# A seventh buffer for expert weights, and another order of layer 0's expert blocks

## What is computed

```python
gi = argmax(softmax(h @ wg + bg)); le = logits of the 8 experts of group gi
tw, ti = top_k(softmax(le), 2); weight = max(pg) * tw / sum(tw); expert = gi * 8 + ti
# for each expert e, over the tokens that chose it, in blocks of 128 rows:
gate, up = split(h[idx] @ w_gu[e], 2)        # 1024 -> 512 + 512
y = (silu(gate) * up) @ w_down[e]            # 512 -> 1024
x = x + g2 * sum over the token's two experts of weight * y
```

## Time and profile before

| | us |
|---|---|
| median of three runs | 2635.58 |
| profiled execution | 2634.51 |
| its span | 2632.6 |
| TensorE matmul busy | 2505.9 (95%) |
| VectorE busy | 1501.1 (57%) |
| POOL busy | 457.7 (17%) |
| matmuls of line 2734: busy, idle before them | 1020.6, 55.4 |
| queue q1, share of 16 engines' span | 51.7% |
| queue q0 | 4.3% |

### The profile page before, as it was taken

The page is one execution under the profiler, slowest core; times in us unless marked ns, Lnnn a source line. Parts: engine busy times, 40 slices in busy tenths (PEclk is TensorE's granted clock), DMA queues, the critical chain, the costliest instruction groups (busy, mean ns, idle before and its releaser), DMA issues.

```text
span 2632.6 us, 33966 instructions
## 1 busy us (share of the span) xinstructions
PE 2505.9 (95%) x12794; PEld 1241.2 (47%) x12794; DVE 1501.1 (57%) x3270; ACT 562.4 (21%) x1181; POOL 457.7 (17%) x527
## 2 busy tenths in 40 slices
PE   6999999999999998999999899999999999999888
PEld 3444456647755533333333344577745433333333
DVE  3264347228778765555555566677787754354435
ACT  3211111118722100000000231488821000000002
POOL 0043200203011132222220012000011122222202
PEclk9999999999999999999999999899999999999999
DMA  9710111114032799999999810300024799999997
GB/s 379 306 26 0 68 49 39 58 22 104 14 142 82 293 392 423 423 382 404 421 408 382 329 49 1 72 2 1 2 75 160 282 402 421 420 413 421 419 406 282
DMA packets 101998, 590.73 MB, mean 224 GB/s; under 512 B 23742, under 2 KB 27078, under 8 KB 76872
## 3 DMA queue, kind: packets, MB, share of 16 engines
q1 hardware_dynamic: 81832, 535.74, 51.7%
q0 software_dynamic: 17408, 43.34, 4.3%
q10 hardware_dynamic: 2592, 9.44, 0.9%
HBM read 555.00 MB, written 45.99 MB: 228 GB/s over the span
## 4 chain that ended last, share of the span: by engine, by line
PE 77%; DMA 14%; DVE 5%; issue 2%; SPq 1%; POOL 0%; ACT 0%; POOLq 0%; DVEq 0%; ACTq 0%
PE PS L2734 28%; PE PS L1072 11%; DMA ar<-in_expert_w_gu_dram 9%; PE PS L1924 5%; PE PS L1268 5%; PE PS L1936 4%; PE PS L1947 4%; PE PS L2157 4%; PE PS L1458 4%; PE PS L1741 4%; DMA ar<-yd 1%; DMA h2d<-ar 1%; PE PS L2150 1%; PE PS L651 1%; DMA ar<-in_ada_w_dram 1%
## 5 line engine op out<-in xcount | busy, mean ns | idle before, releaser
L2734 PE MATMUL PS<-ar 128*32 128x512 f32 (+2 forms) x4608 | 1020.6, 602 | 55.4 <-DMA ar<-in_expert_w_gu_dram 41.9
L2734 PEld LDWEIGHTS PS<-ar 128*32 128x32 f32 (+2 forms) x4608 | 386.3, 138 | 685.5 <-issue 672.2
L1072 PE MATMUL PS<-ar 128*128 128x512 f32 (+1 forms) x768 | 313.9, 565 | 4.2 <-DMA ar<-in_swa_w_in_dram 2.5
L2949 DVE TENSOR_TENSOR ar<-PS,ar 128x512 f32<-128x512 f32 x48 | 33.1, 690 | 485.6 <-ACT ar L2875 485.6
L2963 DVE STREAM_TRANSPOSE ar<-ar 32x128 f32<-32x128 f32 x736 | 296.1, 402 | 10.9
L2875 ACT ACTIVATE ar<-PS 128x512 f32<-128x512 f32 x48 | 28.7, 597 | 1049.8 <-PE PS L2734 1049.8
L1072 PEld LDWEIGHTS PS<-ar 128*128 128x128 f32 x768 | 144.2, 192 | 150.2 <-issue 141.2
L3050 POOL DMA_INDIRECT ar<-h2d,ar x176 | 177.4, 1008 | 140.4 <-DVE ar L2652 57.4
L1980 DVE CUSTOM_DVE_ANT_0 ar<-PS,ar 128x640 f32<-128x640 f32 (+2 forms) x208 | 158.1, 797 | 71.8 <-PE PS L1924 71.7
L2157 PE MATMUL PS<-ar 128*128 128x512 f32 x392 | 175.2, 597 | 1.5 <-ACT ar L2288 0.9
L3058 POOL DMA_INDIRECT yd<-ar x47 | 48.7, 1035 | 711.9 <-DVE ar L2981 699.9
(11 more groups left out here) (349 smaller groups left out, 2452.5 us busy)
## 6 DMA issues: line engine op xcount, KB each, us to landing
ar<-in_expert_w_gu_dram SPq DMA_DIRECT2D x128, 2048.0 KB, 18.2
ar<-in_expert_w_down_dram SPq DMA_DIRECT2D x64, 2048.0 KB, 17.3
ar<-in_ada_w_dram SPq DMA_DIRECT2D x24, 2048.0 KB, 14.7
ar<-yd SPq DMA_DIRECT2D x36, 512.0 KB, 5.6
ar<-in_ab_w_in_dram SPq DMA_DIRECT2D x6, 2048.0 KB, 9.2
h2d<-ar ACTq DMA_DIRECT2D x18, 512.0 KB, 2.8
ar<-in_x_dram SPq DMA_DIRECT2D x8, 512.0 KB, 13.2
ar<-in_ab_w_out_dram SPq DMA_DIRECT2D x1, 4096.0 KB, 30.6
```

What stands on the lines that cost most here:

```text
L1072: mm = nc.tensor.matmul(out_, lhs, rhs, start=(k == 0), stop=(k == KC - 1))
L2734: mm = nc.tensor.matmul(out[at:to], lhsT[:, at:to], w[:, k, cols], start=start, stop=stop)
```

## The change

- `piece_at` gets a seventh buffer at `WR`, where `hb`, `hbT` and a part of `sg` lay. `hb` and `yb` are left with one buffer each, `gub` is dropped and its product is written over `sg`; `yb` lies at `TR`.
- So `gather_quarters(b)` waits for the transpose of b-1 instead of b-2, and `result(b)` for the scatter of b-1 instead of b-2. The gather of block 1 waits until block 0's rows are turned on TensorE. silu waits for the transposes out of `sg` (`guT`) instead of the product (`mul`).
- Layer 0's order becomes WWpqqqWqqqWqqqWpWWWqqqWpW. Layer 1's is unchanged.
- Block 1's down piece is fetched before block 2's gate piece, so seven pieces can be placed by hand (`FIRST`) before the planner takes over; SyncE loads pieces 2 to 5 of layer 0 (1 to 4 before) ahead of the ranks, and 3 to 5 of layer 1 (3 and 4 before).
- The four halves of modulation weights at layer 0's end go into other buffers and wait for other products, in the queue's order: the first one product earlier than before, the second and third one later, the fourth as before. `fix_rows` also waits for the last transpose out of `hb`.

The core of the diff:

```diff
@@ -89,6 +89,10 @@
     rest = [whole(r, 2 + pairs + shared * mains + r - c) for r in range(c, EXP)]
+    if l == 0:
+        take = dict(pair=iter(groups[:pairs]), four=iter(groups[pairs:]), one=iter([[r] for r in rest]))
+        order = ["pair", "four", "one", "four", "one", "four", "one", "pair", "one", "one", "one", "four", "one", "pair", "one"]
+        return first + [x for kind in order for x in next(take[kind])]
     seq = first + groups[0]
@@ -281,16 +285,17 @@
 
-        piece_at = [SLOT1, SLOT1 + 4096, SLOT1 + 8192, SLOT0, SLOT0 + 4096, SLOT0 + 8192]
-        hb = [R(WR + 1024 * i, D) for i in range(2)]
+        piece_at = [SLOT1, SLOT1 + 4096, SLOT1 + 8192, SLOT0, SLOT0 + 4096, SLOT0 + 8192, WR]
+        RING = len(piece_at)
+        FIRST = ((2, 6, 0, 1, 5, 3, 4), (0, 1, 2, 3, 4, 6, 5))
+        hb = R(WR + 4096, D)
         srcq = R(51456, 4 * EXP)
...
         h2q = h2d.rearrange("t (a n) -> (t a) n", a=4)
-        hbT = [R(WR + 2048 + 1024 * i, D).rearrange("p (k n) -> p k n", k=KC) for i in range(2)]
-        sg = [R(WR + 4096 + 512 * i, 512) for i in range(2)]
-        gub = [R(WR + 5120 + 512 * i, 512) for i in range(2)]
+        hbT = [R(WR + 5120 + 1024 * i, D).rearrange("p (k n) -> p k n", k=KC) for i in range(2)]
+        sg = [R(WR + 7168 + 512 * i, 512) for i in range(2)]
         guT = [R(TR + 3072 + 512 * i, 512).rearrange("p (k n) -> p k n", k=4) for i in range(2)]
-        yb = [R(WR + 6144 + 1024 * i, D) for i in range(2)]
+        yb = R(TR, D)
 
...
@@ -348,10 +353,11 @@
                 self.l, self.n = l, f"m{l}"
-                self.blocks, self.pieces, self.at, self.fills = moe_blocks(l), [], {}, [0] * 6
+                self.blocks, self.pieces, self.at, self.fills = moe_blocks(l), [], {}, [0] * RING
                 nb, known = len(self.blocks), {}
                 for b in range(nb + 1):
-                    for part, k in (("g", b), ("d", b - 1), ("u", b)) if l == 1 and b == nb - 1 else (("g", b), ("u", b), ("d", b - 1)):
+                    for part, k in (("g", b), ("d", b - 1), ("u", b)) if l == 1 and b == nb - 1 else (("g", b), ("u", b), ("d", b - 1)) if b != 2 else \
+                            (("d", b - 1), ("g", b), ("u", b)):
                         if not 0 <= k < nb:
@@ -361,7 +367,7 @@
                             self.at.setdefault((part, k), []).append((i, lo, hi))
-                held = [None] * 6
+                held = [None] * RING
 
@@ -369,7 +375,7 @@
                 for i, x in enumerate(self.pieces):
-                    q = min(range(6), key=lambda q: (free_at(q), q))
+                    q = FIRST[l][i] if i < RING else min(range(RING), key=lambda q: (free_at(q), q))
                     self.fills[q] += 1
...
@@ -702,7 +709,7 @@
             nb, n = len(moe.blocks), moe.n
-            for part, b, i, h in (("ga", nb, 0, 0), ("gu", nb, 0, 1), ("gu", nb, 1, 0), ("dn", nb - 1, 1, 1)):
+            for part, b, i, h in (("gu", nb - 1, 0, 0), ("dn", nb - 1, 0, 1), ("ga", nb, 1, 0), ("gu", nb, 1, 1)):
                 sp.wait_ge(*done(f"{n}_{part}", b))
...
@@ -2871,7 +2878,7 @@
                 if b >= 2:
-                    act.wait_ge(*done(f"{n}_mul", b - 1))
+                    act.wait_ge(*done(f"{n}_guT", b - 1))
                 nc.scalar.activation(sg[b % 2], PS[:, 2, :], ACT.Silu).then_inc(S(f"{n}_silu"), 1)
@@ -2937,7 +2944,7 @@
                     dve.wait_ge(*done(f"{n}_gu", b - 1))
-                    V.transpose(hbT[b % 2].rearrange("p k (j m) -> p k j m", j=4), hb[b % 2].rearrange("p (j m k) -> p k j m", j=4, k=KC))\
+                    V.transpose(hbT[b % 2].rearrange("p k (j m) -> p k j m", j=4), hb.rearrange("p (j m k) -> p k j m", j=4, k=KC))\
                         .then_inc(S(f"{n}_hbT"), 1)
...
@@ -2976,9 +2983,9 @@
                 dve.wait_ge(*done(f"{n}_dn", b + 1))
-                if b >= 2:
-                    dve.wait_ge(*done(f"{n}_yo{b % 2}", 16 * (b // 2)))
-                V.tensor_tensor(yb[b % 2], down_out, row, ALU.mult).then_inc(S(f"{n}_y"), 1)
+                if b >= 1:
+                    dve.wait_ge(*done(f"{n}_yo{(b - 1) % 2}", 16 * ((b + 1) // 2)))
+                V.tensor_tensor(yb, down_out, row, ALU.mult).then_inc(S(f"{n}_y"), 1)
 
...
@@ -3037,17 +3044,19 @@
             def gather(b):
+                if b >= 1:
+                    pool.wait_ge(*done(f"{n}_tr", 1))
                 c = moe.blocks[b]["col"]
-                pool.indirect_dma_start(out=hb[b], out_offset=None, in_=h2d,
+                pool.indirect_dma_start(out=hb, out_offset=None, in_=h2d,
                                         in_offset=bass.IndirectOffsetOnAxis(ap=first_i[:, c:c + 1], axis=0),
...
             def gather_quarters(b):
-                pool.wait_ge(*done(f"{n}_hbT", b - 1))
+                pool.wait_ge(*done(f"{n}_hbT", b))
                 c = moe.blocks[b]["col"]
                 for j in range(4):
-                    pool.indirect_dma_start(out=hb[b % 2][:, 256 * j:256 * j + 256], out_offset=None, in_=h2q,
+                    pool.indirect_dma_start(out=hb[:, 256 * j:256 * j + 256], out_offset=None, in_=h2q,
                                             in_offset=bass.IndirectOffsetOnAxis(ap=src4_i[:, 4 * c + j:4 * c + j + 1], axis=0),
@@ -3056,7 +3065,7 @@
                 pool.indirect_dma_start(out=yd, out_offset=bass.IndirectOffsetOnAxis(ap=dst_i[:, c:c + 1], axis=0),
-                                        in_=yb[b % 2], in_offset=None,
+                                        in_=yb, in_offset=None,
                                         bounds_check=2 * TOK - 1, oob_is_err=False).then_inc(S(f"{n}_yo{b % 2}"), 16)
...
@@ -3106,19 +3115,26 @@
                 ada_mid_load(sp, 1)
+                moe.load(sp, 1)
                 sp.wait_ge(*done("o0_h2", 2 * nt))
                 ada_mid_rows(sp)
-                for i in (1, 2, 3, 4):
-                    sp.wait_ge(*done("ada_mm", EARLY + 1 + i // 3))
+                for i in range(2, RING):
+                    if i == 2:
+                        sp.wait_ge(*done("ada_mm", EARLY + 1))
+                    elif i == 5:
+                        sp.wait_ge(*done("ada_mm", EARLY + 2))
+                    elif i == 6:
+                        sp.wait_ge(*done("r0_ord", 1))
                     moe.load(sp, i)
             else:
-                for i in (3, 4):
+                for i in range(3, RING - 1):
                     moe.load(sp, i)
-            sp.wait_ge(*done(f"o{l}_h2", 2 * nt))
-            sp.wait_ge(*done(f"r{l}_ord", 1))
-            for i in range(5, len(moe.pieces)):
+                sp.wait_ge(*done("o1_h2", 2 * nt))
+                sp.wait_ge(*done("r1_ord", 1))
+                moe.load(sp, RING - 1)
+            for i in range(RING, len(moe.pieces)):
                 moe.load(sp, i)
-                if i == 6:
+                if i == RING:
                     sp.wait_ge(*done(f"o{l}_r", nt))
...
```

More of the change, by code:

```diff
@@ L302, in program @@
         ON_DVE = tuple(t for t in range(XT) if t not in ON_PE)
-        fx_a, fx_b, fjunk = hb[1], R(WR + 3072, D), gsel
+        fx_a, fx_b, fjunk = hb, R(WR + 6144, D), gsel
         wdiag = R(8192, 2 * len(ON_PE) * P).rearrange("p (t j n) -> p t j n", t=len(ON_PE), j=2)
@@ L402, in program @@
         kept = {Moe(1).pieces[i]["buf"] for part in "gud" for i, _, _ in Moe(1).at[part, n_blk[1] - 1]}
-        yg[1] += [[R(piece_at[q] + 2048 * h + 1024 * j, D) for j in range(2)] for q in range(6) if q not in kept for h in range(2)]
+        yg[1] += [[R(piece_at[q] + 2048 * h + 1024 * j, D) for j in range(2)] for q in [q for q in range(RING) if q not in kept][:3] for h in range(2)]
         share(("{}_tr",), "m0", "m1", 2)
@@ L407, in program @@
         share(("{}_hbT", "{}_ga", "{}_gu", "{}_silu", "{}_mul", "{}_guT", "{}_dn", "{}_y"), "m0", "m1", n_blk[0])
-        for q in range(6):
+        for q in range(RING):
             share((f"{{}}_w{q}",), "m0", "m1", 16 * Moe(0).fills[q])
@@ L444, in program @@
         share(("{}",), "rpb_in", "ada_late", 16)
+        share(("{}",), "nv_in", "m0_w6", 16 * (XT + 1))
         share(("{}",), "ada_h0", "masks_in", 16)
@@ L2738, in rows_turned @@
             for k in range(KC):
-                tr = nc.tensor.transpose(PS[:, k // 4, (k % 4) * P:(k % 4 + 1) * P], hb[s].rearrange("p (m k) -> p k m", k=KC)[:, k, :], ident)
+                tr = nc.tensor.transpose(PS[:, k // 4, (k % 4) * P:(k % 4 + 1) * P], hb.rearrange("p (m k) -> p k m", k=KC)[:, k, :], ident)
             return tr
@@ L2743, in gated_turned @@
             for k in range(4):
-                tr = nc.tensor.transpose(PS[:, 4, k * P:k * P + P], gub[s].rearrange("p (m k) -> p k m", k=4)[:, k, :], ident)
+                tr = nc.tensor.transpose(PS[:, 4, k * P:k * P + P], sg[s].rearrange("p (m k) -> p k m", k=4)[:, k, :], ident)
             return tr
@@ L2948, in mul @@
                 dve.wait_ge(*done(f"{n}_gu", b + 1))
```

(13 more changed lines are left out.)

6 lines of the change are left out of this document (3 added, 3 removed).

## The result

The changed kernel takes 2645.26 us (median of 20 runs), the kernel before 2635.86 (20 runs): ratio 1.0033, 95% interval 1.0025 to 1.0042. It is slower, by 9.4 us, or a third of a percent; 2647 was forecast. One of the 20 runs of after was a slow one, 14732.61 us at a granted clock of 0.162; the ratio leaves it out, and without it the median is 2644.99. The ratio is estimated from all the other runs of both kernels, so it differs a little from the quotient of the medians.

What follows compares the result with a forecast made beforehand. Two close limits were seen in the expert stages: TensorE's matmuls and, in layer 1, full DMA engines. Layer 0 +10, layer 1 0, the rest +2 gave +12 on 2634.5, with 1.1 to the median: 2647 us, range 2617 to 2664.

Steps and rivals of the forecast that it cites:

- The ring: Loop of transpose, gathers, scatter, landing and result in the expert stages: 23.1 us a turn at full queues, against TensorE's 20.8.
- Rival 1: Expert stages: the ring does not bind, buffer and order give what they can; 2618.5 us, chance 0.22.
- Layer 0's stage: Layer 0's expert stage: 19 ring turns take 431 us, +13.4 us, less 3 for shorter turns, taken as +10.
- 22.0, halfway to 20.8: Layer 0's seven turns of single experts, which want three pieces: 22.0 us each.
- Layer 1: Layer 1's expert stage: ring and weights' stream within 2 us of each other; 0 against before, between -5.4 and +5.
- earlier by that piece, 5.4 us: Layer 1's expert stage: the seventh buffer puts one piece more in flight, 5.4 us once, not for each block.
- I add 6 to the later: Layer 1's expert stage: 6 us added to the later of two close limits, giving 0 against before.
- The start of layer 0: Gather of block 1 waits until block 0's rows are turned: 0 to 4 us a layer, 0.5 taken.
- The ends: Way to layer 1: `result(24)` waits for `scatter(23)`, 0 to 3.7 us, 1.5 taken; later modulation loads called covered.
- rival 3: Whole kernel: gain and ring cancel, turns of 22.0 us, layer 1 -3 to 0; 2633 to 2640 us, chance 0.14.

Runs made afterwards that it cites:

- e1: The changed kernel with scatter(b-4) issued ahead of the four gathers of b on POOL; 2630.52 us.
- e2: The changed kernel with layer 0's piece 3 waiting for the second modulation product, as before the change; the medians differ by 3.6 us, intervals overlapping.
- e8: e3 with the late modulation halves loaded and placed so that only one is left for the last product; 2623.97 us, ratio 0.9952 to before.
- e3: The changed kernel with the edits of e1 and e2 together; 2625.64 us.
- e10: The kernel before, two hb and two yb, with the scatter issued ahead of the gathers; ratio 1.0011 to before.
- e5s: e5 with the scatter issued ahead of the gathers on POOL; 2642.47 us.
- e11: e4 with the scatter issued ahead of the gathers (seven buffers, layer 0's old order); 2630.46 us.
- e5: The kernel before with one hb and one yb and their waits, six buffers, old order; 2649.92 us.
- e4: The changed kernel with layer 0's old block order and old list of late modulation loads, two buffers' places exchanged; ratio 1.0035 to before.
- e9: e8 with the gathers ahead of the scatter again in layer 1 only; time the same as e8's.

## Why the prediction was right, and where it was not

**The ring: right, in every term.** 0.8 + 4.0 + 15.0 + 1.2 + 2.0 us read out of after's trace, a full turn of 23.0 against 23.1 forecast. `result(2)` was put 95.3 us behind the stage's start; it ended 95.8 behind it (1015.02 + 1.22 against 920.4). Rival 1's premise, a scatter that does not feel the gathers ahead of it, is refuted by e1: 13.6 against 10.9 us. The Trainium skill's figure for one such DMA (DMA: Bandwidth & Descriptors, Anatomy of one DMA), 3.2 us for 512 KB, again fits only the shortest landing, 3.3 us. The Trainium skill's sentence that one ring is consumed in order (the same page, Queues, rings and completion order) is said there of the queues of SyncE and ScalarE; e1 agrees with it for GpSimd's q0, where the same scatter lands 2.7 us sooner ahead of the gathers.

**Layer 0's stage: +10 forecast, -2.9 measured.** The step that failed is the turn of the blocks that leave the DMA engines air: "22.0, halfway to 20.8". From `result(2)` to `result(21)` the 19 turns took 410.3 us, not 431: 13 turns of 23.5 on average, and six of 17.5 (18.3, 15.5, 18.5, 18.6, 14.5, 19.7). Five of the six end in the block behind a single expert's, so the forecast had the right kind of block and the wrong price. The shortest turn on VectorE, and the queues in it:

```profile
1343.45 1.23 DVE L2988 TENSOR_TENSOR ar<-PS,ar 128x1024 f32<-128x1024 f32 x1 [6.88 <-DMA yd<-ar]
...
1357.96 1.23 DVE L2988 TENSOR_TENSOR ar<-PS,ar 128x1024 f32<-128x1024 f32 x1 [1.45 <-DMA yd<-ar]
```

```profile
q1 hardware_dynamic: 283, 4.11, 77.0%
q0 software_dynamic: 336, 0.82, 14.4%
```

q1 is at 77.0%, the scatter is there in 5.2 us, and the turn is 14.5. The forecast had bounded such turns from below by TensorE's 20.8. But a ring that is late runs faster than TensorE until it has its slack back; the earlier trace rows gave 19.1 for it, and even that was set aside for TensorE's pace. Only the mean is bounded: 19 x 20.8 = 395.2, and the 15.1 us above it are close to the 15.6 of the stage's waits for "issue". The forecast's ring waits were 559.8 - (549.8 - 13.7) = 23.7 us. e1 prices the ring directly: 10.6.

**Layer 1: 0 forecast, -8.7 in this pair of executions.** All six executions with six buffers have 529.1 to 532.1 us (mean 530.1), all eight with seven 522.6 to 526.3 (mean 525.0), ring closed (524.1) or open (525.9). So the true size is -5.1: the forecast's "earlier by that piece, 5.4 us", one for the stage and not one a block. What failed is "I add 6 to the later": the ring costs nothing there. q1 moves 146.82 MB in 2120 to 2500 us after, against 146.94 in the earlier trace rows, and the ring's 29.6 us of waits stand where 28.2 of waits for weights stood; that fits a pace set by the weights' stream with the ring open or closed. The rest of the -8.7 is spread between executions.

**The start of layer 0: +0.5 forecast, +7.7 measured.** The forecast costed the second gather's new wait, which came to 1.4 us and falls just inside the stage. The wait that came ahead of the stage is the first gather's landing behind three pieces of weights; it follows from SyncE's new order of loads, which is in the diff and which the forecast did not walk. e2 shows it, by 6.5 us of start. What it costs the whole is less: 3.6 us by the medians in after and 4.9 with the ring open, neither clear of noise.

**The ends: +1.5 forecast, +7.1 measured.** `result(24)` waits as named (1469.98, 2.6 us behind its place in before, 1.5 taken):

```profile
1469.98 1.23 DVE L2988 TENSOR_TENSOR ar<-PS,ar 128x1024 f32<-128x1024 f32 x1 [8.66 <-DMA yd<-ar]
```

The wait for the late modulation weights is 2.5 us longer, where nothing was put; little over 1 us of it comes from the list of loads (e8), and the rest goes with the new last blocks, for a reason that is not shown. Behind layer 1 TensorE waits 4.3 us for `yd`, before 2.7 in two waits:

```profile
2608.24 1.37 PE L3263 MATMUL PS<-ar,cst 128*128 128x512 f32 x2 [4.33 <-DMA ar<-yd]
```

This part (+3.0) is not settled: e1 has 1.3 of it and e3 none, while e10, which has two `yb` and two `hb`, has 2.9. It may be spread between executions.

So the total was met by luck: 12.9 us too much for layer 0 and 8.7 too much for layer 1 stood against 7.2 missed at the start, 5.6 at the ends and 3.2 of spread ahead of everything; and the profiled execution lies 4.5 us below the median. In the stages themselves the picture is nearer to rival 3, where gain and ring cancel.

The ring's mechanism is shown. By the medians the change adds up so: single buffers with the ring open +6.3 (e5s against before), the seventh buffer -12.0 (e11 against e5s), the order +0.1 (e1 against e11), the closed ring +14.7 (after against e1), in all +9.1 of the 9.4. The ring alone turns a gain of 5 into a loss of 9. Its price depends on what it holds up: 7.5 us with six buffers (e5 against e5s), 13.5 with seven in the old order (e4 against e11). The first term, 6.3, has no cause shown.

## What to carry to other kernels

When buffers are merged to pay for another, write down the loop of waits that closes, and look at program order inside it: here moving one DMA issue (the scatter ahead of the gathers) was worth 14.7 us, more than the buffer. A loop that binds in some blocks only is to be priced by its mean over many blocks, since its short turns win back what its long ones lose. And walk every queue of the diff at the stage's start and end: loads issued early "for nothing" stood in front of the one gather that everything waited for.

## What was not expected of the hardware

- A gather on q0 (GpSimd's queue) shares badly with q1's backlog: 4.9 us with q1 at 63.4% of the engines (895 to 910 us, before), 11.6 with it at 101.2% (after).
- Layer 1's stage is about as long with some 15 ring waits of at most 2.8 us (mean of four kernels 524.1 us) as with seven to nine waits for gate and up weights of up to 4.5 us (mean of four 525.9). Which waits lower the granted clock could not be read from these runs (0.99 after, 0.98 in e9, with much the same waits).
- Before's own runs spread over 2630.17 to 2645.57 us, and the first 880 us, untouched, differ by 3.2 us between two executions.
